# Modulation products of the second block cut into 48 parts with their weights stationary, run between stages of the first block

## The reference

```python
def adaln(cond, w, b):
    m = jnp.matmul(jax.nn.silu(cond), w) + b
    return jnp.split(m, 3, axis=-1)
def modulated_norm(x, g, shift, scale):
    return rms_norm(x, g) * (1 + scale) + shift
...
    for layer in range(DEPTH):
        shift, scale, gate = adaln(c, w_ada[layer], b_ada[layer])
        c_shift, c_scale, c_gate = adaln(c_ctx, w_ada[layer], b_ada[layer])
        h = modulated_norm(x, norm_g[layer], shift[:, None], scale[:, None])
        ...
        x = x + gate[:, None] * jnp.matmul(y, w_out[layer])
```

## Time and profile before

| | us |
|---|---|
| median of 3 runs (1738.94 to 1742.82) | 1742.74 |
| the profiled execution | 1732.34 |
| its span | 1730.4 |
| TensorE busy | 1610.4 |
| TensorE loading weights | 1242.3 |
| VectorE busy | 970.9 |
| ScalarE busy | 784.7 |

### The profile page before, as it was taken

One profiled execution on the slowest core, in us unless ns is written; L12 is line 12 of the kernel. 1 busy time (PEld: TensorE's weight loads), 2 busy tenths in 40 slices (PEclk: granted clock), 3 DMA queues, 4 the chain that ended last, 5 costly groups with the idle time before them and its releaser, 6 DMA issues.

```text
span 1730.4 us, 20909 instructions
## 1 busy us (share of the span) xinstructions
PE 1610.4 (93%) x8012; PEld 1242.3 (72%) x8012; DVE 970.9 (56%) x1725; ACT 784.7 (45%) x1329; POOL 64.0 (4%) x128
## 2 busy tenths in 40 slices
PE   6999989899989999988999989999969999899997
PEld 5878767899878877767998538677724572776766
DVE  4554557665455544575664336645777631974654
ACT  5446873555344457845553332444410101534552
POOL 4030000000000000000000000000000000400000
PEclk9999999999999999999999999999979999997998
DMA  8763334575545523345765482221110017641100
GB/s 259 241 157 98 122 100 145 138 197 202 191 149 188 177 91 127 100 124 153 193 209 188 160 264 74 75 74 49 53 45 1 25 49 262 183 122 49 49 2 25
DMA packets 174754, 220.94 MB, mean 128 GB/s; under 512 B 6437, under 2 KB 103249, under 8 KB 174588
## 3 DMA queue, kind: packets, MB, share of 16 engines
q1 hardware_dynamic: 171648, 211.65, 38.8%
q0 software_dynamic: 3008, 7.95, 2.3%
HBM read 216.57 MB, written 3.01 MB: 127 GB/s over the span
## 4 chain that ended last, share of the span: by engine, by line
PE 76%; DVE 14%; ACT 6%; issue 3%; DMA 0%; DVEq 0%; ACTq 0%
PE bank L573 19%; PE bank L575 19%; PE bank L574 19%; PE bank L838 5%; PE bank L899 3%; DVE w_low L1490 3%; ACT w_high L1128 2%; PE bank L925 2%; PE bank L910 2%; PE bank L733 1%; PE bank L679 1%; PE bank L710 1%; DVE arena L1807 1%; PE bank L1004 1%; PE bank L684 1%
## 5 line engine op out<-in xcount | busy, mean ns | idle before, releaser
L1490 DVE TENSOR_TENSOR w_low<-raw,w_high 128x1024 fp32r<-128x1024 f32 x352 | 425.0, 1217 | 402.4 <-ACT w_high L1128 401.2
L1128 ACT ACTIVATE w_high<-raw 128x1024 fp32r<-128x1024 f32 x352 | 366.6, 1045 | 344.8 <-PE bank L575 344.8
L573 PE MATMUL bank<-w_high,acts_r 128*128 128x512 f32 (+1 forms) x896 | 359.3, 401 | 29.1 <-DVE acts_r L1650 6.0
L575 PE MATMUL bank<-w_high,acts_r 128*128 128x512 f32 (+1 forms) x896 | 350.0, 391 | 0.0
L574 PE MATMUL bank<-w_low,acts_r 128*128 128x512 f32 (+1 forms) x896 | 348.4, 389 | 0.0
L573 PE MATMUL bank<-acts_r,w_high 128*128 128x256 f32 (+1 forms) x736 | 230.8, 314 | 0.0
L574 PE MATMUL bank<-acts_r,w_high 128*128 128x256 f32 (+1 forms) x736 | 224.2, 305 | 0.0
L575 PE MATMUL bank<-acts_r,w_low 128*128 128x256 f32 (+1 forms) x736 | 224.2, 305 | 0.0
L573 PEld LDWEIGHTS bank<-w_high,acts_r 128*128 128x128 f32 x896 | 172.8, 193 | 69.2 <-DVE w_low L1490 9.3
L575 PEld LDWEIGHTS bank<-w_high,acts_r 128*128 128x128 f32 x896 | 171.8, 192 | 36.3
L574 PEld LDWEIGHTS bank<-w_low,acts_r 128*128 128x128 f32 x896 | 172.3, 192 | 32.2
(11 more groups left out here) (279 smaller groups left out, 1825.5 us busy)
## 6 DMA issues: line engine op xcount, KB each, us to landing
raw<-in_w_in SPq DMA_DIRECT2D x70, 1024.0 KB, 5.2
raw<-in_w_up SPq DMA_DIRECT2D x64, 512.0 KB, 5.5
raw<-in_w_down SPq DMA_DIRECT2D x32, 1024.0 KB, 4.9
raw<-in_w_ada SPq DMA_DIRECT2D x24, 1024.0 KB, 5.3
raw<-in_w_in SPq DMA_DIRECT2D x32, 512.0 KB, 5.1
raw<-in_w_o SPq DMA_DIRECT2D x8, 1024.0 KB, 5.1
raw<-in_w_out SPq DMA_DIRECT2D x8, 1024.0 KB, 5.0
raw<-in_w_out_c SPq DMA_DIRECT2D x4, 768.0 KB, 5.4
```

Of the source, the lines that this page charges most:

```text
L573: mm(o, lh, rh, start=start, stop=False)
L575: return mm(o, ll, rh, start=False, stop=stop)
L1128: run(A_(high, src, ACT.Copy), (high_ready, n + 1))
L1490: run(V.tensor_tensor(low, src, high.bitcast(F32), ALU.subtract), (split_ready, n + 1))
```

## The change

The modulation of both layers is computed in 48 parts, each two of the eight row blocks of 512 columns of `w_ada`: eight products with 128 x 128 weights stationary and two columns of `cond` moving, into 8 columns of one bank. VectorE copies the first of four parts into `ada_t` and adds the other three, so the result lies in columns at once. The places: 21 parts of the first layer (13 in attention units of odd number; 2 each behind the output transposes, behind the turning of the merged rows, before the second norm's transposes and behind them), 19 of the second (2 before and 2 behind the first norm's transposes, 8 in units 9 to 23, then 2, 2, 2 and 1), and 8 between the down products and norm 5's transposes. The weights come on GpSimd's queue (512 KB each) into the context tiles of `X`, later into two mask areas and three work areas; the context itself is loaded after part 34. The silu of the conditions moves to the first layer. Bias and gain are two passes of VectorE over columns, after norm 5 has been finished. `modulation(1)` on TensorE is gone. `gate_rows` uses a gate column, repeated, as stationary operand and the identity as moving one. SP's list loses its `ada` halves, and `in2` quarters are no longer held back. ScalarE squares the context tiles of norm 5 before it waits for the block's result.

```diff
+ADA = 3 * KD
+ADA_PARTS = LAYERS * 24
+def ada_places():
+    return [n % 2 for n in range(35)] + [2 + n % 2 for n in range(5)] + [3, 2, 4, 5, 6, 3, 2, 4]
+def ada_in_attention(l, u):
+    return u % 2 == 1 and (l == 0 or 9 <= u <= 23)
...
-        slabs += [("ada", l, c) for c in range(6)] + [("in2", l, c) for c in range(7)]
+        slabs += [("in2", l, c) for c in range(7)]
         slabs += [("out2", l, c) for c in range(2)]
...
         hg = carve(at, 4, N4)
-        gate_row_at = at[0]
-        gate_row = carve(at, D)
-        fourier_at = at[0]
+        at[0] += D
         fourier_fwd = carve(at, 2, 2, SEQ)
...
+        def ada_is_loaded(n):
+            places = ada_places()
+            return ada_loaded[places[n]], 16 * places[:n + 1].count(places[n])
+        def ada_before(n):
+            places = ada_places()
+            return max((m for m in range(n) if places[m] == places[n]), default=None)
...
                 while self.n < len(quarters) and (self.n < SPLITS or position[self.n - SPLITS] <= p):
-                    name, l = quarters[self.n][:2]
-                    if name == "in2" and position["ada", l, 5] >= p:
-                        return
                     self.one(self.n)
...
+            ada_next = [0]
+            def ada_parts(count, among=ANY_BANK):
+                for _ in range(count):
+                    n = ada_next[0]
+                    ada_next[0] += 1
+                    if n == 0:
+                        pe.wait_ge(*cond_ready_s.at("done"))
+                    pe.wait_ge(*ada_is_loaded(n))
+                    w = ada_raw[ada_places()[n]].rearrange("p (k n) -> p k n", k=2)
+                    o = open_bank("ada", n, among=among)
+                    for f in range(4):
+                        for kk in range(2):
+                            ins = mm(o[:, 2 * f:2 * f + 2], w[:, kk, f * P:(f + 1) * P], cond[:, n % 4 * 2 + kk, :],
+                                     start=kk == 0, stop=kk == 1)
+                    close_bank(ins, "ada", n)
             pe.wait_ge(first_loaded, 2 * 16)
...
+                    ada_parts(2)
                 norm_transposes(2 * l, xn1, TILES, 2)
+                if l:
+                    ada_parts(2)
                 turned = [("qT", l, 0, b) for b in range(6)] + [("qT", l, 1, b) for b in range(6)]
                 for c in range(9):
...
                     advance(filler, 1000 if u >= len(U) else 3 if U[u][0] == "A" else 4)
+                    if u < len(U) and ada_in_attention(l, u):
+                        ada_parts(1, ATTENTION_BANKS)
                     if u >= 2:
                         values(u - 2)
...
                     close_bank(ins, "oT", l, b)
+                ada_parts(2)
...
                     if k == 4:
                         turn_merged(1)
+                        ada_parts(2)
...
+                ada_parts(2)
                 norm_transposes(2 * l + 1, xn1, TILES, 2)
+                ada_parts(1 if l else 2)
...
-            def modulation(l, row):
-                pe.wait_ge(*cond_ready_s.at("done"))
-                for c in range(6):
-                    o = open_bank("ada", l, c)
-                    for k in range(KD):
-                        n = half_at["ada", l, c, k // 4]
-                        if k % 4 == 0:
-                            pe.wait_ge(*half_is_loaded(n))
-                        w = raw[:, n % SLOTS, k % 4 * 512:(k % 4 + 1) * 512]
-                        ins = mm(o[0:2, :], cond[:, k, :], w, start=k == 0, stop=k == KD - 1)
-                    close_bank(ins, "ada", l, c)
-                    half_used[half_at["ada", l, c, 0]] = half_used[half_at["ada", l, c, 1]] = filled("ada", l, c)
-                for c in range(6):
-                    pe.wait_ge(*emptied("ada", l, c))
-                o = open_bank("adaT", l)
-                for k in range(16):
-                    ins = tr(o[:, 2 * k:2 * k + 2], row[0:2, k * P:(k + 1) * P], ident[0:2, 0:2])
-                close_bank(ins, "adaT", l)
...
+            def gate_rows(l, sequences):
+                pe.wait_ge(*ada_ready.at(l))
                 for s in range(sequences):
                     for c in range(2):
                         o = open_bank("gateB", l, s, c)
-                        ins = mm(o[:, :], select[:, s, :], row[0:2, c * 512:(c + 1) * 512], start=True, stop=True)
+                        for k in range(4):
+                            gate = ada_t[:, l, 2 * KD + 4 * c + k, s:s + 1].to_broadcast([P, P])
+                            ins = mm(o[:, k * P:(k + 1) * P], gate, ident[:, :], start=True, stop=True)
                         close_bank(ins, "gateB", l, s, c)
...
-            modulation(0, ada_row)
+            ada_parts(8)
+            assert ada_next[0] == ADA_PARTS
             norm_transposes(5, xn2, T4, 1)
...
-            modulation(1, ada_row3)
-            gate_rows(1, ada_row3[:, 2 * D:3 * D], 1)
+            gate_rows(1, 1)
             norm_transposes(6, xn3, T4, 1)
...
+            def norm_guess(n, tiles, xn, added=None, last=(), until=None):
+                for t in [t for t in range(tiles) if t not in last] + list(last):
+                    if last and t == last[0]:
+                        act.wait_ge(*until)
...
+                if l == 0:
+                    act.wait_ge(cond_loaded, 2 * 16)
+                    run(A_(cond_e[:, :, :], cond[:, :, :], ACT.Exp, scale=-1.0), cond_exp.by(0))
...
-            act.wait_ge(*x_added.at(4))
             act.wait_ge(context_loaded, 16)
-            norm_guess(5, T4, xn2)
+            norm_guess(5, T4, xn2, last=(0, 1), until=x_added.at(4))
...
+            def take_ada(count):
+                for _ in range(count):
+                    n = ada_taken[0]
+                    ada_taken[0] += 1
+                    at = n // 4 % 6 * 4
+                    dst = ada_t[:, n // 24, at:at + 4, :]
+                    part = bank("ada", n)[:, 0:8].rearrange("p (f s) -> p f s", f=4)
+                    dve.wait_ge(*filled("ada", n))
+                    if n % 4 == 0:
+                        run(V.tensor_copy(dst, part), emptied("ada", n))
+                    else:
+                        dve.wait_ge(*emptied("ada", n - 1))
+                        run(V.tensor_tensor(dst, dst, part, ALU.add), emptied("ada", n))
...
+                if l:
+                    take_ada(2)
+                else:
                     dve.wait_ge(first_loaded, 2 * 16)
                 norm_evacuate(2 * l, 0, l)
...
+                if l == 0:
+                    dve.wait_ge(*cond_exp.at(0))
...
+                    if u < len(U) and ada_in_attention(l, u):
+                        take_ada(1)
...
-            def modulation(l, row, gate, bias):
-                dve.wait_ge(ada_loaded, 16)
-                if l:
-                    dve.wait_ge(ada_bias_loaded, 16)
-                for c in range(6):
-                    cols = slice(c * 512, (c + 1) * 512)
-                    dst = row[0:2, cols] if c < 4 else gate[0:2, (c - 4) * 512:(c - 3) * 512]
-                    splits.due("ada", l, c)
-                    dve.wait_ge(*filled("ada", l, c))
-                    run(V.tensor_tensor(dst, bank("ada", l, c)[0:2, :], bias[0:2, cols], ALU.add), emptied("ada", l, c))
-                dve.wait_ge(*filled("adaT", l))
-                run(V.tensor_copy(ada_t[:, :, :], bank("adaT", l)[:, 0:32].rearrange("p (k s) -> p k s", k=16)), emptied("adaT", l))
-                run.settle()
-                run(V.tensor_scalar(gain[:, :, :], ada_t[:, KD:2 * KD, :], 1.0, None, ALU.add))
+            def modulation(l):
...
+                b = ada_bias[:, l, :].unsqueeze(2).to_broadcast([P, ADA, 2])
+                run(V.tensor_tensor(ada_t[:, l], ada_t[:, l], b, ALU.add))
+                run.settle()
+                run(V.tensor_scalar(gain[:, :, :], ada_t[:, l, KD:2 * KD, :], 1.0, None, ALU.add))
                 run.settle()
                 g = g_cols[:, 2, l, :].unsqueeze(2).to_broadcast([P, KD, 2])
                 run(V.tensor_tensor(gain[:, :, :], gain[:, :, :], g, ALU.mult), ada_ready.by(l))
...
-            modulation(0, ada_row, gate_row, ada_bias)
+            take_ada(5)
             norm_finish(5, T4, xn2)
-            modulated_evacuate(5, mod_tmp)
+            take_ada(3)
+            modulation(0)
+            modulated_evacuate(5, 0, mod_tmp)
+            modulation(1)
...
-            modulation(1, ada_row3, ada_row3[:, 2 * D:3 * D], ada_bias3)
             norm_finish(6, T4, xn3)
-            modulated_evacuate(6, mod_tmp3)
+            modulated_evacuate(6, 1, mod_tmp3)
...
+            for l in range(LAYERS):
+                loads.append((ada_bias[:, l, :], A["b_ada_2"][l].rearrange("(k p) -> p k", p=P)))
...
+                pool.dma_start(cond[:, :, 0], A["c_2"][0].rearrange("(k p) -> p k", p=P)).then_inc(cond_loaded, 16)
+                pool.dma_start(cond[:, :, 1], A["c_ctx_2"].rearrange("(k p) -> p k", p=P)).then_inc(cond_loaded, 16)
+            def load_ada(n):
```

(31 more changed lines are left out.)

## The result

The changed kernel takes 1753.27 us (median of 20 runs, 1742.43 to 1767.19), the kernel before, measured beside it, 1739.63 (20 runs, 1731.42 to 1747.91): a ratio of 1.0084, 95% interval 1.0063 to 1.0105. It is slower, by about 14 us.

The account below looks back on a forecast made before the run. TensorE, busy 93% of the span and 76% of the last-ending chain, was taken as the bound. 1732.3 - 68 saved + 47 for parts + 36 for clock = 1747, plus 10.4 for the median: 1757 us, range 1696 to 1774.

Parts of the forecast that it names:

- the likeliest case: Whole kernel: the clock falls at many parts and the kernel takes 1745 to 1780 us; chance 0.50.
- Removed, second place: Block's last products to norm 6's transposes: transposes start at 1437.2 instead of 1472.9, 35.7 us, plus 3.5 for splits: 39.2 saved.
- Removed, first place: Down products to norm 5's transposes: 47.2 us becomes 22, plus 3.5 for splits: 28.7 saved, 36 if the clock holds.
- Rival 4: The two places do not shorten, norm 5 waiting above all for parts 45 to 47 from GpSimd's queue; chance, with others, 0.02.
- Price of a part: TensorE, each of 48 parts: 16 weight loads at 0.11 us, 1.8 us a part, 86 us in all; bounds 1.05 and 1.95.
- Rival 3: Two-column products go at L845's rate, parts of 1.1 us: 1686, median 1696 us; chance 0.05.
- The clock: First block: falls at two of three attention parts, 14 x 2.3 = 32 us, plus 4 behind norm transposes: +36.
- the 735.3 stretch: Profile of the kernel before, 735.3 to 738.7: TensorE ran 64-column products and waited, then the clock went from 1.00 to 0.50.
- Rival 1: The clock holds through the parts: 1694, median about 1705 us; chance 0.27.
- rival 2: The clock falls at only 5 or 6 of 21 attention parts, 13 us, and 22 us first place: median about 1735; chance 0.16.
- The crossing: Number of clock falls at which gain turns to loss: over some 13 falls of 2.3 us the change is slower, below faster.
- The parts in the first block: 40 parts added: +35 in attention, +3.2 behind output transposes and turned merge, +9 behind norm transposes; sum +47 us.

Follow-up runs that it names:

- the 128-column run: Changed kernel with the two condition columns repeated 64 times, so 128 columns stream behind each weight load of the parts: 1707.51 us, ratio 0.9821.
- the old address: Changed kernel with an unused tile of 576 bytes ahead of the arena, which starts at 105280 again: 1741.93 us, ratio 1.0021.
- 32 columns: Changed kernel with the two condition columns repeated 16 times as moving operand of the parts: 1732.94 us, ratio 0.9993.
- the run with the address alone: Kernel before with two small tiles (576 bytes) put behind the arena, which so starts at 104704: 1749.05 us, ratio 1.0074.
- its two padded twins: Changed kernel with 128 moving columns and an unused tile ahead of the arena: 64 bytes (104768) 1697.5 us, 0.9777; 576 bytes (105280) 1702.22 us, 0.9765.
- the kernel at 105344: Kernel before with an unused tile of 64 bytes ahead of the arena: 1733.01 us, ratio 0.9972.

## Why the prediction was right, and where its sum was not

The forecast, 1757 us and slower, lies 4 us above the measured 1753.27, and the likeliest case's own range, 1745 to 1780, holds it. The whole range, 1696 to 1774, holds a clear gain as well as a clear loss, and "slower" had a chance of 0.48, so the agreement tells little. And the sum behind it lacked a term as large as the whole result, and another error covered it.

- **Removed, second place.** Forecast: transposes at 1437.2, with products that end at 1424.9. The trace of the kernel before has their end at 1425.6, so this is 11.6 us, and 11.6 us were measured (12.0 counted from the last product's start, as in the table). All of the 35.7 us came.
- **Removed, first place.** Forecast 22 us, three parts at full clock and five at half; measured 24.5 with the clock at 0.57 (24.1 counted from the products' end, as the forecast was), 14.5 when it holds (14.4 in the forecast). Six parts ran at half clock, not five, and took 3.4 us each, not 3.3. The norm was later than the 13.9 us I gave it, because its first Newton step queued on VectorE behind the fetching of a part: ScalarE was done at 1083.7, and VectorE took up the norm at 1087.57, right behind L1548.

```profile
1083.48 0.20 ACT L1138 ACTIVATE nstat<-nstat 128x4 f32<-128x4 f32 x1
...
1087.49 0.17 DVE L1548 COPY ada_t<-bank 128x8 f32<-128x8 f32 x1 [3.25 <-PE bank L652]
1087.57 0.16 DVE L1501 TENSOR_SCALAR nstat<-nstat 128x4 f32<-128x4 f32 x1
```

  It cost nothing: TensorE had parts until 1097.5. With the stages behind the two places (4.1 and 3.9 us shorter, where I had 3.5 each) 66.7 us were saved, 68 foreseen. The 4.1 and 3.9 are no test of the 3.5: these two stages of the kernel before change by +2.7 and -9.2 us when only its arena is moved, the second with 24 us less at half clock. Rival 4's late transfer did not come: TensorE runs through all 128 products.
- **Price of a part.** 1.8 us forecast; a part in the attention is 16 weight loads in 1.99 us, the last one included to its end, one every 0.119, so 1.8 to 1.9:

```profile
185.26 1.99 PEld L652 LDWEIGHTS bank<-cond,X 128*128 128x128 f32 x16
```

  Rival 3 (L845's rate, 0.066) is refuted. The Trainium skill (TensorE: Matmul & The Clock Gate, LDWEIGHTS) has a load go by its columns, about P/1.2 ns, which makes an estimate of 107 ns for 128; at full clock the loads of a part start 112 to 119 ns apart here, near it and a little above.
- **The clock.** Forecast: 14 falls in the attention, +36 us in the first block. The trace has 12 falls there (1 before) and 119 us at half clock in the first block against 41; at the 0.38 us for each that the 128-column run gives, this is 30 us, and at the most 39. That the clock falls in most parts was right, and it is the step with the least behind it: "the nearest row is the 735.3 stretch, which fell". The price of a fall was too high: the attention has 54 us more at half clock for 11 more falls, 1.9 us lost for each by the 0.38 and not 2.3, so 21 us in place of 32; the other 9 lie in stages that the forecast gave 4. Rival 1 is refuted by the trace, and rival 2 (5 or 6 falls) by the number of falls, though the 21 us lie between its 13 and my 32. The crossing that I gave, some 13 falls, was worked out wrongly: with 21 us of gain before the first fall and 2.3 us for each it is at 9. That rival 1 would have been a win is shown too: with the clock held the kernel took 1707.5, where the forecast said about 1705, and 1702.2 and 1697.5 in the two kernels with another address.
- **The clock over all executions.** Every run lists its granted clock. Within the kernels (154 runs, each set of runs about its own mean) a us more at half clock goes with 0.41 us more time (standard error 0.02), within the 20 runs of the changed kernel with 0.39 (0.04); so the 0.38 holds up. The mean time at half clock is 205 us in the changed kernel (185 to 233), 210 with the old address and 137 in 63 runs of the kernel before; the changed kernel's trace, with 224, is one of its slower executions. So the falls cost it 26 to 28 us on average, where the forecast had 43: 36 in the first block and 7 at the first place. Brought to one half-clock time (130 us, at 0.38) the means are, as estimates, with the arena at 104704, 1725.5 for the changed kernel, 1725.0 with 128 and 1726.5 with 32 columns, against 1749.6 for the kernel before; at 105280 they are 1711.8 (1716.6 with 128 columns) against 1735. What the change moves is thus worth 18 to 24 us with the clock set aside; the forecast had 28, 75 less 47.
- **The parts in the first block.** Forecast +47. The block grew by 94.3. Less 30 for the clock and 16 for the address (the run with the address alone: the first block 22.4 longer, with 17 us more at half clock, which at 0.38 are 6), 48 are left. This is a difference of estimates, but no other term is asked for.
- **What was missing.** "With the clock as before the change would give 1711" assumed that what the change does not touch keeps its speed. The tiles' sizes moved the arena, and all split products of the kernel start some per cent farther apart: about 13 us by the run of the address alone (1749.05 to 1736.09; the two had the same time at half clock on average, 129 and 132 us), and by the changed kernel with the old address 0.6% (from 1.0084 to 1.0021, with an uncertainty of 0.4, each against the kernel before measured beside it).
- **What covered it.** The sum gave 1747 for the profiled execution, and that took 1759.9, 13 more. The step from there to the median, +10.4, is the second wrong one: it is taken from the kernel before, whose profiled execution was a fast one (1732.3; 20 runs have 1739.6). That of the changed kernel lay 6.6 above its own median. The two errors, 13 too little and 17 too much, nearly cancel. Told by differences, which need no step to the median, it is the same: the forecast's +15 was -28 and 43 for the clock; measured was about -24, 26 for the clock and 14 for the address, which the sum did not have (the means of the two kernels differ by 16 us, their medians by 14). The clock's term, too large by some 17 us, covered the address.

So the side, "slower", came out for a reason that was not in the prediction. Without the shift of the address the change is at 1.0021 (0.9988 to 1.0055): no difference that was measured. The removed work and the added parts with their clock are even there (1741.93 to 1737.97), where the sum had them 15 us apart.

**What stays open.** Why the address sets the products' distance, and what chooses between 113 and 118 at one address. Found with the arena at 105280 and 104768: 113 or 118 with 229 or 233 ns; at 104704, in all seven traces: 119 to 120 with 232; at 105344: 120 with 227. Whether the products' distance is the whole of the 13 us was not shown: the kernel at 105344 has 120 ns in its MLPs and was not slower, with the time at half clock made equal either (1735.2 to 1734.8).

## What to carry to other kernels

Before work is moved into an engine's idle places, ask what it does to the clock there. A stretch of weight loads with two columns behind each is busy by every count and was still followed by half clock; repeating the moving columns cost nothing (eight parts took 14.5 us at full clock with 128 columns, as many as forecast for 2), and turned a loss of 0.8% into a gain of 1.8% at the same addresses (2.2 and 2.4% in its two padded twins, the fastest kernels of this study).

When a change alters the size of any tile, compare the addresses of the tiles behind it, and measure the kernel before at the new addresses. Here that control alone, 1.0074, was as large as the result.

Do not add to the forecast of one kernel the distance of another kernel's profiled execution from its median.

## What the runs showed of the hardware that I had not expected

- Products that follow each other without a wait, at full clock, with the same operand sizes, start 113 to 120 ns apart (256 columns) and 227 to 233 (512 columns), mostly in patterns that repeat every three or five products (in the changed kernel 115, 118, 122, 120, 119), for a whole stage. The Trainium skill (TensorE: Matmul & The Clock Gate, Back-to-back issue gap) gives N/2.4 + 2.5 ns at 2.4 GHz for a product by itself; the estimate from it is 109 and 216, and no stage here reached it.
- The distance changed when the tile of the activations, the moving operand in one form and the stationary one in the other, was moved: by 64 bytes from 113 and 229 to 120 and 227 ns, by 576 bytes to 119 or 120 and 232. At one address it takes two values, 113 and 118.
- Time at half clock cost 0.38 to 0.41 us for each us, less than half of it.
- With 128 columns in the parts the first block had 17 us at half clock, fewer than the 41 of the kernel before. None is left from the end of attention 0 to norm 2 (20 before), where eight parts stand at what were TensorE's waits and two behind the transposes. That filling the waits is what keeps the clock there was not tested by itself.
